# Layer joins of a two-block transformer on one Trainium2 core: sums of squares on VectorE, token halves at eight joins, two spare weight slots, one slab moved

## The reference

```
def rmsnorm(x, g):
    xf = x.astype(jnp.float32)
    y = xf * lax.rsqrt(jnp.mean(xf * xf, axis=-1, keepdims=True) + EPS)
    return (y * g.astype(jnp.float32)).astype(x.dtype)

def modulate(x, g, shift, scale):
    return rms_norm(x, g) * (1 + scale) + shift

def half_ffn(x, g, shift, scale, gate, w13, w2):
    return x + 0.5 * gate * swiglu(modulate(x, g, shift, scale), w13, w2)
...
        x = x + conv_ffn(rmsnorm(x, norm_ffn[i]), ffn_w_up[i], ffn_conv_w[i], ffn_conv_b[i], ffn_w_down[i])
```

## Time and profile before

| | us |
|---|---|
| median of 3 runs | 3765.01 |
| lowest, highest | 3763.18, 3766.81 |
| the profiled execution | 3767.65 |
| its span, first to last instruction | 3765.8 |
| TensorE busy in the span | 3576.8 (95%) |
| VectorE, ScalarE, GpSimd busy | 1697.4, 1181.4, 1183.5 |

### The profile page before, as it was taken

How to read it: one execution, slowest core, us unless ns; L and a number is a source line. 1 busy time by engine, 2 the same in 40 slices (tenths; PEclk the granted TensorE clock), 3 DMA queues, 4 the chain that set the end, 5 groups by cost and what they waited for, 6 DMA issues and landing times.

```text
span 3765.8 us, 44727 instructions
## 1 busy us (share of the span) xinstructions
PE 3576.8 (95%) x16544; PEld 2911.4 (77%) x16544; DVE 1697.4 (45%) x1897; ACT 1181.4 (31%) x1410; POOL 1183.5 (31%) x609
## 2 busy tenths in 40 slices
PE   6989999999998999998999989899999999979999
PEld 5856788868886888897788766678877887767887
DVE  2344685532335856444664455366443244232222
ACT  3423342242324433433222234322222222332221
POOL 2201222231113222454443341244334333334332
PEclk8956999999999999998999989999999999999999
DMA  3200343321112434354454320145432243212222
GB/s 134 79 23 12 113 150 120 117 99 56 56 45 96 142 125 140 117 185 146 162 195 142 126 77 1 45 162 193 141 120 86 91 145 117 90 68 78 97 93 90
DMA packets 69659, 402.43 MB, mean 107 GB/s; under 512 B 7296, under 2 KB 9872, under 8 KB 30864
## 3 DMA queue, kind: packets, MB, share of 16 engines
q1 hardware_dynamic: 46176, 318.79, 23.9%
q10 hardware_dynamic: 23344, 81.73, 6.3%
HBM read 398.39 MB, written 2.10 MB: 106 GB/s over the span
## 4 chain that ended last, share of the span: by engine, by line
PE 91%; DVE 4%; ACT 2%; POOL 2%; issue 1%; DMA 0%; DVEq 0%; ACTq 0%; POOLq 0%
PE banks L333 24%; PE banks L334 24%; PE banks L335 24%; PE banks L372 2%; PE banks L441 2%; PE banks L348 2%; PE banks L349 2%; PE banks L347 2%; POOL h_lo L1642 2%; DVE stg L1122 2%; PE banks L665 1%; PE banks L421 1%; PE banks L656 1%; PE banks L405 1%; ACT h_hi L759 1%
## 5 line engine op out<-in xcount | busy, mean ns | idle before, releaser
L1621 POOL TENSOR_TENSOR wlo<-raw,whi 128x512 fp32r<-128x512 f32 x299 | 771.8, 2581 | 2016.0 <-ACT whi L717 1988.5
L333 PE MATMUL banks<-h_hi,whi 128*128 128x512 f32 (+1 forms) x3144 | 1210.4, 385 | 90.6 <-POOL h_lo L1642 82.4
L334 PE MATMUL banks<-h_lo,whi 128*128 128x512 f32 (+1 forms) x3144 | 1195.7, 380 | 0.0
L335 PE MATMUL banks<-h_hi,wlo 128*128 128x512 f32 (+1 forms) x3144 | 1195.4, 380 | 0.0
L717 ACT ACTIVATE whi<-raw 128x2048 fp32r<-128x2048 f32 x297 | 567.4, 1910 | 708.7 <-PE banks L335 705.6
L333 PEld LDWEIGHTS banks<-h_hi,whi 128*128 128x128 f32 x3144 | 597.8, 190 | 227.9 <-issue 85.5
L1104 DVE TENSOR_TENSOR wlo<-raw,whi 128x1536 fp32r<-128x1536 f32 x297 | 548.6, 1847 | 351.3 <-ACT whi L717 351.3
L334 PEld LDWEIGHTS banks<-h_lo,whi 128*128 128x128 f32 x3144 | 598.4, 190 | 112.9 <-issue 5.3
L335 PEld LDWEIGHTS banks<-h_hi,wlo 128*128 128x128 f32 x3144 | 597.5, 190 | 112.1
L333 PE MATMUL banks<-mid_hi,whi 128*128 128x512 f32 (+1 forms) x1232 | 471.9, 383 | 0.8 <-POOL wlo L1621 0.8
L334 PE MATMUL banks<-mid_lo,whi 128*128 128x512 f32 (+1 forms) x1232 | 467.1, 379 | 0.0
(11 more groups left out here) (241 smaller groups left out, 2886.9 us busy)
## 6 DMA issues: line engine op xcount, KB each, us to landing
raw<-stream SPq DMA_DIRECT2D x299, 1024.0 KB, 4.8
mraw<-mod_stream ACTq DMA_DIRECT2D x144, 512.0 KB, 3.4
x<-xT SPq DMA_DIRECT2D x1, 2048.0 KB, 14.1
out<-x SPq DMA_DIRECT2D x1, 2048.0 KB, 7.1
ka<-k_a ACTq DMA_DIRECT2D x1, 1600.0 KB, 6.7
ko<-k_odd ACTq DMA_DIRECT2D x1, 1152.0 KB, 5.2
crow<-c_rows ACTq DMA_DIRECT2D x1, 1024.0 KB, 10.5
cx<-ctxT SPq DMA_DIRECT2D x1, 1024.0 KB, 7.2
```

Of the source, the lines that this page charges most:

```text
L333: mm(o, hi, a_hi[:, kc, 0:T], start=(kc == 0), stop=False)
L334: mm(o, hi, a_lo[:, kc, 0:T], start=False, stop=False)
L335: last = mm(o, lo, a_hi[:, kc, 0:T], start=False, stop=(kc == K - 1))
L1621: G.tensor_tensor(wlo[:, slot, WD:], raw[:, slot, WD:], whi[:, slot, WD:].bitcast(F32), ALU.subtract)\
```

## The change

1. The squares are added on DVE. ACT writes the first square to a new tile `ss` and the others to the two buffers `sq`; DVE adds them (`add_square`), and TensorE makes one float32 matmul for a norm, or one for each token half.
2. At eight joins (cffn0, mix1, cffn1, m01, m02, m10, m11, m12) the last two slabs of the round and the first two slabs of the next stage run in halves of 256 tokens. The second halves of the last two slabs go to the banks `aux[2]` and `aux[3]`. The next two slabs are split into slots of their own, `xhi` and `xlo`, before the last two slabs are done.
3. All norms work in units of 256 tokens through four half buffers; `h_lo` of a norm is made on DVE, and the shift goes into the ACT copy and the DVE subtraction. POOL keeps the splits of weights, of `mid` and of mixer outputs.
4. m00 is scaled ahead of the last round of ctx_ffn, not behind it. ctx1 is normed into `cx` early in ffn00, and the slab ctx_kv is multiplied behind the five slabs of a_in. `adapt` (the small tables of the modulated norms) moves ahead of the last round.
5. The context tokens are loaded 22 slabs earlier. The output is stored as eight DMAs of a chunk each. ACT loads its function table ahead of use at six joins.

```diff
+HALVED = {"cffn0": ("even_out", 0, "conv0"), "mix1": ("conv0", 30, "odd_in0"), "cffn1": ("odd_out", 0, "conv1"),
+          "m01": ("ffn00", 30, "a_in"), "m02": ("a_out", 0, "ffn01"), "m10": ("ffn01", 30, "ffn10"),
+          "m11": ("ffn10", 30, "c_in"), "m12": ("c_out", 0, "ffn11")}
...
 # TensorE
+            def stat(norm, k):
+                cnt = len(SUMS[norm]) - 1
+                a, b = (0, TOKENS[norm]) if norm not in HALVED else (k * HS, k * HS + HS)
+                pe.wait_ge(sum_done, SUM_AT[norm] + (7 if norm in HALVED and k == 0 else cnt))
...
+            def first_pair(norm, js0=(0, 1)):
...
+                for i in range(2):
+                    slab_split(n0 + i)
+                for kc in range(DC):
+                    unit_ready(norm, kc)
+                    for i in range(2):
+                        half_out(n0 + i, kc, DC, js[i], h_hi, h_lo, 0)
+                    if norm in HALVED and kc == 4:
+                        stat(norm, 1)
+                for i in range(2):
+                    for kc in range(DC):
+                        if i == 0:
+                            unit_ready(norm, 8 + kc)
+                        last = half_out(n0 + i, kc, DC, js[i], h_hi, h_lo, HS)
+                    last.then_inc(slab_done, 1)
+
+            def halved(norm, a_hi, a_lo, K, split0):
+                s0 = slab_of(*HALVED[norm][:2])
+                for i in range(2):
+                    slab_out(s0 + i, (s0 + i) % 2, a_hi, a_lo, K, S, split0=split0 if i == 0 else None)
+                for i in (2, 3):
+                    slab_split(s0 + i)
+                    for kc in range(K):
+                        last = half_out(s0 + i, kc, K, (0, 1), a_hi, a_lo, 0)
+                    last.then_inc(half_done, 1)
+                for i in (2, 3):
...
+                    last.then_inc(slab_done, 1)
+                    if i == 2:
+                        stat(norm, 0)
+                first_pair(norm)
...
 # ScalarE
+            def halved(norm, then=None):
+                s0 = slab_of(*HALVED[norm][:2])
+                for i in range(2):
+                    split_next(s0 + i)
+                    square(norm, 2 * i)
+                    square(norm, 2 * i + 1)
+                for i in range(2):
+                    split_extra(s0 + 4 + i)
+                load_ln_exp()
+                for k in range(4, 8):
+                    square(norm, k)
+                inverse(norm, 0)
...
 # VectorE
+            def halved(norm, gate):
...
+                for i in range(2):
+                    split_extra(s0 + 4 + i)
+                for i in (2, 3):
+                    residual_half(s0 + i, r, gate, True, halves + i - 1)
+                    add_square(norm, 2 * i)
+                    add_square(norm, 2 * i + 1)
...
 # conv1 and ctx_ffn, VectorE
+                adapt([(0, 0, 0, 1), (1, 0, 1, 1), (2, 0, 0, 0), (3, 0, 1, 0)], [(0, 0, 0, 1), (1, 0, 0, 0)])
+                for k in range(1, 8):
+                    add_square("ctx0", k)
+                units("ctx0")
...
+            ffn("ctx_ffn", "swiglu", CTX, 0, 0, early=lambda: units("m00"))
+            last_round("ctx_ffn", CTX, 0, "ctx1")
...
 # SyncE
+            for c in range(DC):
+                sp.wait_ge(x_written, written(("ffn11", 2), c))
+                sp.dma_start(out[c * P:(c + 1) * P, :], x[:, c, :]).then_inc(stored, 16)
```

More of the change, by code:

```diff
@@ L63, with written @@
     for _j in range(_k):
[L64 to L75, removed]
+        ROUND[_name, _j], ROUND_BEFORE[_name, _j] = _n, _prev
+        _n, _prev = _n + (12 if (_name, _j) in HALVED_ROUNDS else 8), (_name, _j)
+def written(r, c, first_half=False):
+    return ROUND[r] + c + 1 + (4 if r in HALVED_ROUNDS and c >= 4 and not first_half else 0)
 SPLIT = {}
 _n = 0
-for _name, _k in [("mix0", 8), ("even", 8), ("cffn0", 8), ("conv0", FC), ("mix1", 8), ("odd", 4), ("cffn1", 8),
-                  ("conv1", FC), ("ctx0", 8), ("ctx_ffn", FC), ("ctx1", 8), ("m00", 8), ("ffn00", FC), ("m01", 8),
-                  ("a", 8), ("m02", 8), ("ffn01", FC), ("m10", 8), ("ffn10", FC), ("m11", 8), ("c", 8), ("m12", 8),
+for _name, _k in [("mix0", 16), ("even", 8), ("cffn0", 16), ("conv0", FC), ("mix1", 16), ("odd", 4), ("cffn1", 16),
+                  ("conv1", FC), ("ctx0", 8), ("ctx_ffn", FC), ("m00", 16), ("ffn00", FC), ("m01", 16),
+                  ("a", 8), ("m02", 16), ("ffn01", FC), ("m10", 16), ("ffn10", FC), ("m11", 16), ("c", 8), ("m12", 16),
                   ("ffn11", FC)]:
@@ new lines, in halved @@
+            def halved(norm, then=None):
[10 more added lines that the diff above has]
+                inverse(norm, 0)
+                square(norm, 8)
+                square(norm, 9)
+                for u in range(4):
+                    unit_hi(norm, u)
+                square(norm, 10)
+                square(norm, 11)
+                for u in range(4, 8):
+                    unit_hi(norm, u)
+                inverse(norm, 1)
+                for u in range(8, 16):
+                    unit_hi(norm, u)
+                    if u == 13 and then is not None:
+                        A(small[:, 63:64], par[:, PC["eps"]:PC["eps"] + 1], then)
@@ L1679, in _ @@
             splits(slab_of("odd_out"), 4)
[L1680 to L1681 removed]
+            ffn("conv1", S)
             ffn("ctx_ffn", CTX)
[L1683 removed]
+            ffn("ffn00", S)
+            splits(slab_of("a_in"), 5)
             splits(slab_of("ctx_kv"), 1)
[L1685 to L1689 removed]
+            projections_taken(pool, "ctx_kv")
             pool.wait_ge(stage_loaded, 80)
```

599 lines of the change are left out of this document (381 added, 218 removed).

## The result

| | before | after |
|---|---|---|
| median, us | 3765.91 (4 runs) | 3651.16 (4 runs) |
| lowest, highest | 3763.18, 3767.16 | 3646.66, 3653.17 |
| span of the profiled execution | 3765.8 | 3648.8 |
| TensorE busy | 3576.8 | 3490.0 |

After over before is 0.9694 (95% interval 0.9679 to 0.9708). The forecast was 3661 us, range 3624 to 3699.

A forecast was written before the change was run, and what follows sets the result against it. TensorE's work plus its waits bound the kernel (busy 3576.8 of 3765.8 us). Gains of 73 + 8.5 + 3 + 14 + 1 + 4 = 103.5 us gave 3664.2, less 2.6 to the median: 3661 us, range 3624 to 3699.

The forecast's parts named there:

- The joins: Eight joins of two stages: loss falls from 143 us to 70 with fewer sums and halved slabs, gain 73 us.
- Halving: At each join, 256-token steps of 0.12 us, two for one of 0.2275, cost 1.8 to 2.4 us.
- The waits: TensorE before the fourth slab and first sum: K=8 0.4 us, K=6 0.9 and 4.2, K=4 2.2 and 6.9.
- The clock: Clock loss after long waits at joins: 1 us for each K=6 join, 2.5 us for cffn1.
- The third slab: Next stage's third slab, weights late by about 1 us at cffn0 and cffn1, 0.4 behind two Gelu; 2.4 in all.
- The clock's rule of thumb: Half clock followed 4.33 us of idle time, full clock 3.71; a 4.2 us wait lies between and may cost clock.
- DVE instead of GpSimd: Low part moved to DVE: POOL's spare split would not delay residuals; otherwise about 1.1 us more per join, left out.
- The start: Kernel start: squares no longer paced by TensorE's sums, low parts sooner; gain 8.5 us, bounds 4 and 12.
- The end of ctx_ffn: Last round of ctx_ffn: loss falls from 33.7 to 19.7 us, gain 14, bounds 5 and 28.
- DVE's pace of every join: Rival, all joins: DVE operations and hand-overs cost 0.15 us more each, about +34 us, 3695 us; chance 0.26.
- the first sum does not wait: Rival, joins: load or splits run 4 us ahead of the count, about -30 us, 3631 us; chance 0.17.
- Slower than before: Rival, eight joins: half clock from the first sum through the halved pair, 184 us lost, 3845 us; chance 0.03.

The follow-up runs named there:

- 4 runs: Not a follow-up kernel: the count of timed runs behind each median, 3765.91 us for the kernel before and 3651.16 us for the changed kernel.
- late_spare: Changed kernel with the second spare slot's split moved behind the squares and additions of the first token half, at all eight joins: 3618.7 us.
- m00_pairs: Changed kernel with m00's units spread behind slabs 26 to 32 of ctx_ffn, scalings ahead of VectorE's weight split, low parts behind it: 3640.8 us.
- pool_lo: Changed kernel with the low parts of the four norms without a shift (mix0, cffn0, mix1, cffn1) on GpSimd again: 3652.5 us.
- no_prefetch: Changed kernel without ScalarE's early load of the next stage's function table at six joins: 3652.8 us.
- ctx0_early: Changed kernel with ctx0's squares and additions one round earlier in conv1, its sum unmoved in TensorE's list: 3642.3 us.
- sums_only: Kernel before, with only the squares added on VectorE and one float32 matmul per norm; no halves or spare slots: 3775.5 us.
- both_late: Changed kernel with both spare slots' splits behind the squares and additions of the first token half: 3627.7 us.

## Why the prediction was right, point by point

**The joins.** Mechanism and size held (74.7 against 73): the list order on ScalarE and VectorE makes the first sum late at K=6 and K=4, and late_spare removed exactly that. That the size held so well is partly luck, since several terms were wrong and offset each other. At m10 six undisturbed slabs take 3 x 8.40 + 3 x 10.88 = 57.8 us; the join took 67.5, a loss of 9.7 against 9.6 forecast. Its terms:

*Halving* was taken as 2.1 to 2.4 us a join. In late_spare 31 steps of 256 tokens take 3.62 us, 0.1168 each:

```profile
2729.80 0.28 PE L384 MATMUL banks<-h_hi,xhi 128*128 128x256 f32 x1
...
2733.42 0.28 PE L385 MATMUL banks<-h_lo,xhi 128*128 128x256 f32 x1
```

Two of them are 0.0069 us over the step of 10.88/48 = 0.2267, so 96 matmuls of the next pair cost 0.7 us. In the round a K=6 slab takes 8.40 us, 0.2333 a matmul; 68 steps of its halves (2706.01 to 2714.05) take 8.05, 0.1183 each, so its two slabs cost 0.2 us more. That is 0.9 us at a K=6 join, not 2.1. The step of 0.12 read off two rounded rows was too coarse, and so was the 0.2275, for which two rounded rows give 0.23. TensorE: Matmul & The Clock Gate (the Trainium skill, section Back-to-back issue gap) had given an estimate of 0.5 us; the trace is nearer to it than to my figure.

*The sum* of 256 tokens was right at 0.43 us. In late_spare's rows the second weight matmul behind it starts at 2714.72, 0.67 us behind the one at 2714.05; without the sum two steps make 0.24. Half of the cost lies in the slow step from 2714.41 to 2714.72.

*The waits* with K=6 were taken as 0.9 and 4.2 us: 0.83 and 3.5 to 4.4. With K=4, 2.2 and 6.9: 2.21 and 5.60. With *K=8*, 0.4 each: 2.02, 0.3 and 1.30 us at cffn0, m02 and m12. *Single units* were taken as 0.5 to 1.0 us a join and wait 0.2 at most.

*The clock* was taken as 1 us at K=6 and cost some 1.7, and 2.6 at mix1. At cffn1 it was taken as 2.5: half clock lasted 4.2 us behind the long wait and 3.4 behind the wait of 2.21, which makes 3.8.

*The third slab*: waits of 0.86 us at cffn0 and cffn1 and 0.41 at m11, for 1, 1 and 0.4. The 5.5 us of that paragraph is 5.3 by its own terms (0.6 + 1.91 + 2.8), which changes nothing.

**The clock's rule of thumb failed.** From 4.33 us with half clock and 3.71 without I expected the wait's length to decide. At cffn0 the wait was only 2.02 us, and the granted clock was 0.50 from 373.35 to 376.77 (m00_pairs, pool_lo and no_prefetch waited 0.8 to 1.2 us there, ctx0_early 1.72, and kept full clock). The wait of 2.21 us at cffn1 was followed by half clock in the changed kernel (1127.70 to 1131.11), and the same wait in late_spare was not. All waits of 3.5 us and more at the joins were followed by it.

**DVE instead of GpSimd.** The prediction left GpSimd's part of the spare split out of the residuals' time, and the rows agree: at 2734.63 two residuals take 0.87 us beside GpSimd's split (2733.00 to 2735.84). The scalings and additions, which read two SBUF operands, are held: 1.90 and 2.55 us for two. SBUF — State Buffer (the Trainium skill, section Who interferes with whom) says so of both kinds, one input in SBUF and two, and the trace agrees. I applied it to the residuals alone. The credit that the start's sum gave to the low part off GpSimd (1 us for the first unit, 3 for the pace) was misplaced: in pool_lo, with the low part back on GpSimd, the start is 0.2 us longer.

**The start** gained 11.5, not 8.5. The sums give 3.7 of it (sums_only), for which 4.5 was taken. The other 7.7 us come with whatever else changed there: units of 256 tokens and the halved pair are what is left once pool_lo has excluded GpSimd's pace. No run split it further.

**ctx0**: 3.0 as forecast; the wait is 9.45 us. **The end of ctx_ffn**: idle times of 0.82 and 12.80 us against 0.8 and 14.5, gain 17.6 against 14, inside its bounds. **a_in**: 1.8 against 1. **Output**: 5.05 against 4, inside 0 to 7.1; the store of one chunk lands in 2.0 us. **Not foreseen**: three waits of 0.98 us in the slabs up of ctx_ffn, where the marks lose 2.3 us. They come behind m00's inverse root and the two table loads around it (1536.34 to 1541.78), now in ScalarE's list there. That these are the cause is not shown: no run took them away.

**The rivals.** DVE's pace of every join is excluded (four waits of 0.2 us at most for a unit's low part). That the first sum does not wait was wrong of this kernel; late_spare is that case, and its gain of 32.5 us matches the 30 that the rival was priced at. *Slower than before* is excluded too: half clock lasted 3.4 us behind the wait at most joins, at most 5.2, and not through the halved pair.

## What to carry to other kernels

When work is moved to another engine, read what stands ahead of it in that engine's list: the same additions lost 8 us or gained 21 by their place around one weight split. Work taken off TensorE is worth nothing while TensorE must wait for the same result on another engine. A chain counted in this way, step by step from the trace, held to 0.1 us at m10, and it also names the next edit: whatever in it the waited-for result does not need can go behind it. Put VectorE's operations with two SBUF operands where GpSimd is idle, and price small steps from many rows, not from two.

## What the hardware showed unexpectedly

- Half clock came behind 2.02 us of idle time at cffn0 and not behind 3.71 us at another place; behind 2.21 us at cffn1 in one kernel and not in another. The wait's length alone does not tell.
- The even mixer, with the same code in nine kernels, took 160.3 us with 116 us of it at half clock and up to 166.8 with 136.5.
- GpSimd's 128x512 split takes 2.84 to 2.86 us when VectorE's 128x1536 split has just started, and 1.71 at m10 beside VectorE's additions, which took 3.47 us for two there in place of 1.49. VectorE's split takes 1.76 when it starts first, and 4.52 for two in a row in both_late, where the second starts beside GpSimd's first: in these rows whoever comes second waits.
